# Splitting the heads while the recurrent stage still runs, the second norm made inside the output products, and first weights fetched ahead

## What is computed

```python
def _modulate(x, g, shift, scale):
    return _rmsnorm(x, g) * (1 + scale) + shift

def _hgrn_readout(o, gate, norm_g, w_out):
    o = _rmsnorm(o, norm_g)                       # per head
    o = o.reshape(o.shape[0], o.shape[1], E_WIDTH).astype(gate.dtype)
    return (o * jax.nn.silu(gate)) @ w_out        # 2048 -> 1024

def first_block(x, c, ...):
    ...
        x = x + gate[:, None] * y                 # y: the readout
    ...
        h = _modulate(x, norm_g[i], shift[:, None], scale[:, None])
    ...

def _conv_mixer(h, w_in, b_in, ...):
    p = h @ w_in + b_in                           # 1024 -> 3 * 2048
    a, gl, gate = jnp.split(p, 3, axis=-1)
    u = a * jax.nn.sigmoid(gl)
    ...
```

## Time and profile before

| | |
|---|---|
| median of 3 runs (lowest, highest) | 3842.87 us (3842.66, 3844.66) |
| the profiled execution | 3843.6 us |
| its span in the trace | 3841.7 us |
| PE busy in the span | 3545.6 us |
| mean granted clock of PE | 0.959 |

### The profile page before, as it was taken

The page is one execution under the profiler, slowest core; times in us unless marked ns, Lnnn a source line. Parts: engine busy times, 40 slices in busy tenths (PEclk is TensorE's granted clock), DMA queues, the critical chain, the costliest instruction groups (busy, mean ns, idle before and its releaser), DMA issues. The chain is left out here.

```text
span 3841.7 us, 57188 instructions
## 1 busy us (share of the span) xinstructions
PE 3545.6 (92%) x24387; PEld 2545.6 (66%) x24387; DVE 2026.4 (53%) x3153; ACT 1306.6 (34%) x2188; POOL 598.5 (16%) x316
## 2 busy tenths in 40 slices
PE   8999999997899989899999999999897978999998
PEld 5778778775444437554555547888575867878886
DVE  4157877773198885712133335333567575065422
ACT  4146665663211124521133223332343122333331
POOL 0000000002000000200000004444530001434442
PEclk9999999998999999999799999999898979999999
DMA  7622221222456560332021033332320002323332
GB/s 271 211 69 53 79 53 53 73 59 78 120 183 187 178 197 23 106 66 48 14 58 44 17 96 96 98 99 72 81 71 2 4 2 52 98 83 93 97 91 71
DMA packets 517587, 331.11 MB, mean 86 GB/s; under 512 B 31356, under 2 KB 493749, under 8 KB 517078
## 3 DMA queue, kind: packets, MB, share of 16 engines
q1 hardware_dynamic: 517334, 327.45, 29.5%
HBM read 316.93 MB, written 10.49 MB: 85 GB/s over the span
## 5 line engine op out<-in xcount | busy, mean ns | idle before, releaser
L1383 PE MATMUL cv_bank<-hT,cv_w 128*128 128x512 f32 x768 | 343.7, 601 | 13.7 <-DMA cv_w<-in_conv_w_in_dram 13.7
L3685 POOL TENSOR_TENSOR tl_wl<-tl_w,tl_wh 128x1024 fp32r<-128x1024 f32 (+1 forms) x104 | 246.2, 2368 | 679.0 <-ACT tl_wh L3798 678.8
L1534 DVE SCALAR_TENSOR_TENSOR conv_u<-cv_pad,vec,conv_u 128x512 f32<-128x512 f32 x480 | 319.2, 742 | 0.0
L1383 PEld LDWEIGHTS cv_bank<-hT,cv_w 128*128 128x128 f32 x768 | 143.3, 191 | 194.6 <-issue 180.2
L2498 POOL TENSOR_TENSOR mp_wl<-mp_w,mp_wh 128x1024 fp32r<-128x1024 f32 x72 | 173.1, 2407 | 592.9 <-ACT mp_wh L2572 592.9
L3798 ACT ACTIVATE tl_wh<-tl_w 128x1024 fp32r<-128x1024 f32 (+1 forms) x104 | 108.5, 1043 | 332.1 <-PE tl_bank L3722 329.9
L797 PE MATMUL hg_bank<-hg_hh,hg_wh 128*128 128x512 f32 x512 | 207.8, 406 | 4.6 <-PEq L194 4.6
L799 PE MATMUL hg_bank<-hg_hh,hg_wl 128*128 128x512 f32 x512 | 203.2, 397 | 0.0
L798 PE MATMUL hg_bank<-hg_hl,hg_wh 128*128 128x512 f32 x512 | 202.9, 396 | 0.0
L3720 PE MATMUL tl_bank<-tl_room,tl_wh 128*128 128x512 f32 x464 | 183.8, 396 | 11.7 <-POOL tl_wl L3685 10.9
L3722 PE MATMUL tl_bank<-tl_room,tl_wl 128*128 128x512 f32 x464 | 182.5, 393 | 0.0
(11 more groups left out here) (745 smaller groups left out, 8267.0 us busy)
## 6 DMA issues: line engine op xcount, KB each, us to landing
cv_ada<-in_w_ada_dram SPq DMA_DIRECT2D x48, 1024.0 KB, 7.7
hg_w<-in_hgrn_w_in_dram SPq DMA_DIRECT2D x64, 512.0 KB, 7.0
mp_w<-in_w_mlp_dram SPq DMA_DIRECT2D x64, 512.0 KB, 4.2
open_w<-in_ada_w_dram SPq DMA_DIRECT2D x12, 2048.0 KB, 9.8
cv_w<-in_conv_w_in_dram SPq DMA_DIRECT2D x48, 512.0 KB, 4.1
tl_w<-in_w_ffn_in_dram SPq DMA_DIRECT2D x44, 512.0 KB, 4.0
fr_w<-in_w_in_dram SPq DMA_DIRECT2D x26, 512.0 KB, 3.8
at_w<-in_w_in_dram SPq DMA_DIRECT2D x24, 512.0 KB, 4.0
```

Of the source, the lines that this page charges most:

```text
L1383: ins = pe.matmul(ps[n % RING][:, :], W[n % SLOTS][:, k * P:(k + 1) * P], K.hT[:, k, :], start=(k == 0), stop=(k == KD - 1))
L1534: ins = dve.scalar_tensor_tensor(o, x, by, o, ALU.mult, ALU.add)
L3685: pool.tensor_tensor(WL[u % SPLIT][:, 0:n, :], W[u % RAW][:, 0:n, :], WH[u % SPLIT][:, 0:n, :].bitcast(F32), ALU.subtract).then_inc(low, 1)
```

## The change

The splitting of heads 0 to 13 goes into hgrn_phase's last turn: ACT makes the high parts in three groups (`heads_high`) and POOL the low parts, into `ho_rh` and into the places of `hg_hl` and `ho_rl`. The weights of the first output tile are fetched in that stage too, ahead of SP's wait for the last projection. A new stage, heads_out_phase, takes the place of stream_phase("ho") and of norm_phase: it splits the first weights in four parts and the heads 14 and 15, makes the 8 output tiles as before, and beside them squares the new residual tiles (ACT) and adds the squares up (DVE), so that two matmuls with ones are left at its end, then the logarithm and the exponential. The scaling and the shift go to the start of conv_phase, one tile at a time, and the first product waits for each tile (`h_ok`). The convolution's first four weight tiles go to buffers of their own (`cv_first`), fetched in heads_out_phase behind the third output tile's weights.

```diff
@@ hgrn_phase, SP
+                sp.dma_start(K.hoW[:, :, :], inp["hgrn_w_out"][0].rearrange("(k p) n -> p k n", p=P)[:, :, 0:P]).then_inc(K.ho_in, 16)
                 sp.wait_ge(proj, NG * NH)
@@ hgrn_phase, POOL
+                for h in range(SPLIT_HEADS):
+                    pool.wait_ge(r_high, h + 1)
+                    o = K.hgL[:, h, :] if h < KD else K.hoL[:, h - KD, :]
+                    pool.tensor_tensor(o, hO[:, h, :], K.hoH[:, h, :].bitcast(F32), ALU.subtract).then_inc(r_low, 1)
@@ hgrn_phase, ACT
+                def heads_high(a, b):
+                    for h in range(a, b):
+                        act.wait_ge(fin_ok, h + 1)
+                        act.activation(K.hoH[:, h, :], hO[:, h, :], ACT.Copy).then_inc(r_high, 1)
...
                     log(1, h - 1)
+                    if h == NH:
+                        heads_high(0, 4)
...
                     turn(0, h - 1)
+                    if h == NH:
+                        heads_high(4, 9)
                     exps(1, h - 1)
+                    if h == NH:
+                        heads_high(9, SPLIT_HEADS)
...
-def stream_phase(K, tag, w, x, kt, iters, col, on_act, on_dve, freed_by, start=None):
...
+CONV_FIRST = [EW, 0, EW + P, P]
+def heads_out_phase(K):
+    SPLIT, BANKS, PARTS, ITERS = 2, 6, 4, KD
+    STEP = NH // PARTS
...
+                for u in range(1, ITERS):
+                    if u == 2:
+                        sp.wait_ge(part_low, PARTS)
+                    elif u > 2:
+                        sp.wait_ge(low, u - 2)
+                    sp.dma_start(W[u % 2][:, :, :], w[:, :, u * P:(u + 1) * P]).then_inc(w_in[u % 2], 16)
+                    if u == 2:
+                        sp.wait_ge(r_low, 2)
+                        for n, at in enumerate(CONV_FIRST):
+                            sp.dma_start(K.cvW[:, n, :].rearrange("q (k n) -> q k n", n=P), wc[:, :, at:at + P]).then_inc(K.cv_in, 16)
...
+                pe.wait_ge(added, KD - 1)
+                pe.matmul(SUM[:, :], K.ones[:, :], acc[:, :], start=True, stop=False)
+                pe.wait_ge(squared, KD)
+                pe.matmul(SUM[:, :], K.ones[:, :], sq[:, (KD - 1) % 2, :], start=False, stop=True).then_inc(sum_ok, 1)
...
+                act.wait_ge(K.ho_in, 16)
+                for c in range(PARTS):
+                    act.activation(WH[0][:, STEP * c:STEP * (c + 1), :], W[0][:, STEP * c:STEP * (c + 1), :], ACT.Copy).then_inc(part_high, 1)
+                for k in range(NH - 2, NH):
+                    act.activation(RH[:, k, :], K.hO[:, k, :], ACT.Copy).then_inc(r_high, 1)
+                weights_high(1)
+                act.preload_act_table_set(LOG_EXP_SET)
+                for u in range(ITERS):
+                    act.wait_ge(freed, u + 1)
+                    if u >= 2:
+                        act.wait_ge(added, u - 1)
+                    act.activation(sq[:, u % 2, :], K.xT[:, u, :], ACT.Square).then_inc(squared, 1)
                     weights_high(u + SPLIT)
...
@@ conv_phase, PE, ACT, DVE
                         for k in range(KD):
-                            ins = pe.matmul(ps[n % RING][:, :], W[n % SLOTS][:, k * P:(k + 1) * P], K.hT[:, k, :],
+                            if n == 0:
+                                pe.wait_ge(h_ok, k + 1)
+                            ins = pe.matmul(ps[n % RING][:, :], slot(n)[:, k * P:(k + 1) * P], K.hT[:, k, :],
...
+                for k in range(KD):
+                    act.wait_ge(h_mul, k + 1)
+                    act.activation(K.hT[:, k, :], K.hT[:, k, :], ACT.Identity, bias=K.mod[:, SHIFT + k, 0:1]).then_inc(h_ok, 1)
...
+                for k in range(KD):
+                    dve.scalar_tensor_tensor(K.hT[:, k, :], K.xT[:, k, :], gain[:, k:k + 1], K.hT[:, KD - 1, :],
+                                             ALU.mult, ALU.mult).then_inc(h_mul, 1)
...
-    norm_phase(K, [(K.xT, K.hT, T, K.at["norm_g"] + 8, 24, 32, 0)])
```

More of the change, by code:

```diff
@@ L130, in open_phase @@
         K.ctxL = K.sb(under, "ctx_hl", [P, KD, TC], F32R)
+    with ExitStack() as under:
+        K.hoL = K.sb(under, "ho_rl", [P, NH - KD, T], F32R)
     K.ctxT = K.sb(K.early, "ctxT", [P, KD, TC])
@@ L134, in open_phase @@
         slots = [K.sb(under, f"open_w{i}", [P, KD, GC]) for i in range(2)]
+    with ExitStack() as under:
+        K.cvW = K.sb(under, "cv_first", [P, len(CONV_FIRST), KD * P])
     K.hO = K.sb(K.early, "hgrn_out", [P, NH, T])
+    with ExitStack() as under:
+        K.hoH = K.sb(under, "ho_rh", [P, NH, T], F32R)
+    K.ho_in, K.cv_in = (K.ctx.enter_context(nc.semaphore(name)) for name in ("ho_first", "cv_first"))
     K.heads = ExitStack()
@@ L711, in hgrn_phase @@
          at_ok, kv_ok, s_ok, out_ok, sq_ok, ms_ok, ln_ok, rs_ok, o1_ok, fin_ok, back_ok) = sems[5:31]
-        high, low, x_back, half_ok = (K.ctx.enter_context(nc.semaphore(f"hg_sem{n}")) for n in range(4))
+        high, low, x_back, half_ok, r_high, r_low = (K.ctx.enter_context(nc.semaphore(f"hg_sem{n}")) for n in range(6))
+        SPLIT_HEADS = NH - 2
         GROUPS = [(ZF, 0), (ZF, 1), (ZB, 0), (ZB, 1), (Q, 0), (G, 0)]
@@ L1185, in weights_high @@
                 def weights_high(u):
-                    if u >= iters:
+                    if u >= ITERS:
                         return
-                    act.wait_ge(w_in[u % RAW], 16 * (u // RAW + 1))
+                    act.wait_ge(w_in[u % 2], arrived(u))
                     if u >= SPLIT:
                         act.wait_ge(summed, u - SPLIT + 1)
[L1191 to L1202, removed]
+                    act.activation(WH[u % SPLIT][:, :, :], W[u % 2][:, :, :], ACT.Copy).then_inc(high, 1)
+                act.wait_ge(K.ho_in, 16)
+                for c in range(PARTS):
+                    act.activation(WH[0][:, STEP * c:STEP * (c + 1), :], W[0][:, STEP * c:STEP * (c + 1), :], ACT.Copy).then_inc(part_high, 1)
@@ L1215, in _ @@
-                if start:
-                    start(dve, own)
-                for u in range(iters):
-                    if freed_by == "dve":
-                        dve.wait_ge(summed, u + 1)
-                    else:
-                        dve.wait_ge(freed, u + 1)
-                    on_dve(dve, u, ps[u % BANKS], freed, own)
+                for c in range(PARTS):
+                    dve.wait_ge(part_high, c + 1)
+                    part = slice(STEP * c, STEP * (c + 1))
+                    dve.tensor_tensor(WL[0][:, part, :], W[0][:, part, :], WH[0][:, part, :].bitcast(F32), ALU.subtract).then_inc(part_low, 1)
@@ new lines, in _ @@
+                for k in range(NH - 2, NH):
+                    dve.wait_ge(r_high, k - NH + 3)
+                    dve.tensor_tensor(RL(k), K.hO[:, k, :], RH[:, k, :].bitcast(F32), ALU.subtract).then_inc(r_low, 1)
+                for u in range(ITERS):
+                    dve.wait_ge(summed, u + 1)
+                    dve.scalar_tensor_tensor(K.xT[:, u, :], ps[u % BANKS][:, :], K.mod[:, 16 + u, 0:1], K.xT[:, u, :],
+                                             ALU.mult, ALU.add).then_inc(freed, 1)
+                    if u < KD - 1:
+                        dve.wait_ge(squared, u + 1)
+                        if u == 0:
+                            dve.tensor_copy(acc[:, :], sq[:, 0, :]).then_inc(added, 1)
+                        else:
+                            dve.wait_ge(added, u)
+                            dve.tensor_tensor(acc[:, :], acc[:, :], sq[:, u % 2, :], ALU.add).then_inc(added, 1)
@@ L1286, in conv_phase, with slot, landed @@
         ada_in = (ada_in0, ada_in1)
+        h_gain, h_mul, h_ok = (K.ctx.enter_context(nc.semaphore(f"conv_h_sem{n}")) for n in range(3))
+        def slot(n):
+            return K.cvW[:, n, :] if n < NF else W[(n - NF) % SLOTS][:, :]
+        def landed(n):
+            return (K.cv_in, 16 * NF) if n < NF else (w_in[(n - NF) % SLOTS], 16 * ((n - NF) // SLOTS + 1))
         grid = lambda t: t.rearrange("q (r t) -> q r t", t=GW)
@@ L1329, in _ @@
                         if n < 3 * NT_ + NT_:
[L1330 removed]
+                            if n >= SLOTS + NF:
+                                load(n)
                             n += 1
```

105 lines of the change are left out of this document (53 added, 52 removed).

## The result

The changed kernel takes 3823.84 us (median of 5 runs, 3822.29 to 3827.77) against 3842.66 (5 runs of the kernel before on the same chip, 3839.22 to 3844.66): a ratio of 0.9949, 95% interval 0.9938 to 0.9961. It is 0.5% faster. The profiled run took 3823.84, its span is 19.6 us shorter than before.

What follows compares the result with a forecast made beforehand. PE, busy 92% of the span, was taken as the bound, so only its waits could be won: 3843.6 - 10.6 - 19.7 + 9 = 3822.3 us, range 3814 to 3830.

Steps and rivals of the forecast that it cites:

- Norm and convolution's start: From last output product to first convolution product: 6.1 us instead of 25.75, as norm work is hidden; gain 19.7 us.
- Output projection's start: Heads already split and first weights fetched: PE starts about 1.3 us after the stage's start, not 11.89; gain 10.6 us.
- the two meet: Output projection: second tile's weights ready at 14.1 us, just as the first tile ends at 14.2, so no wait.
- The tail: Head 15 to the stage's end: POOL's low parts hold DVE, loss about 9 us, from 29.2 to 38 us.
- every second boundary: In head 15, POOL gets in at half of DVE's boundaries: 8 subtractions go ahead, at 1.1 us each.
- The upper bound of 13.7: Rival for head 15: POOL gets in at each DVE boundary, 13.7 us lost, 3827.0 us in all; chance 0.26.
- both slow starts: First output tile kept at 12.9 us and first convolution product 2.5 us slow, since PE's clock falls in waits.
- the main case: Whole kernel: loss of 6 to 12 us in head 15, time 3819 to 3826 us; chance 0.40.
- the wait of 4.5 us: Sign: PE's wait before the first output product should be some 4.5 us.
- three signs of being wrong: DVE's instructions as short as before, POOL running past DVE's last instruction, or the second output tile waiting for its weights.
- The rival without early start: Convolution's own weights come late, so only 10.6 us is won and 9 given back: 3842.0 us; chance 0.04.
- the slow one: Each POOL subtraction holds DVE far longer; at 2.85 us each, 39.9 us lost and 3853.2 us; chance 0.03.

Runs made afterwards that it cites:

- e5: The changed kernel with the convolution's first four weights loaded at the convolution's start again; 3833.85 us, ratio 0.9974.
- e6: The changed kernel's norm and convolution alone, with heads split and first weights loaded at the output projection's start as before the change; 3820.06 us, ratio 0.9942.
- e8: e1 plus the second output tile's weights fetched in head 15 and unread PE products filling PE's waits; 3809.95 us, ratio 0.9912.
- e1: The changed kernel with the heads' fourteen low parts made by DVE in its own waits of head 15 instead of by POOL; 3813.62 us, ratio 0.9924.
- e2: The changed kernel with POOL's fourteen subtractions released at three moments when DVE reads PSUM or waits; 3815.20 us, ratio 0.9930.
- e3: The changed kernel with each of POOL's fourteen subtractions made as two of 256 columns; 3822.59 us, ratio 0.9949.
- e4: The changed kernel with all sixteen heads split by ACT and DVE at the output projection's start, not in the tail; 3820.07 us, ratio 0.9945.
- e9: e8 with PE's unread products placed closer to the output projection's start, and one fewer at the convolution's start; 3811.35 us, ratio 0.9917.

## Why the prediction was right, step by step

The time came out 1.5 us above the forecast, inside the range, but that it came so close is luck: terms cancel. With the working's terms against the measured ones:

- **Norm and convolution's start**: 19.7 forecast, 19.6 measured; the 6.1 us were 6.15. Shown, by e5 and e6.
- **Output projection's start**: 10.6 forecast, 8.8 measured. PE did start 1.4 us after the stage's start. The first tile then took 13.5 us instead of 12.9 and ended at 14.92 instead of 14.2, and the step "the two meet" failed by a little: the second weights landed 8.6 us after the stage's start (916.93 - 908.32), not 7.6, since the DMA took 6.8 us from issue to landing and not 5.87 (why, no run shows); POOL ended at 923.51, PE waited 0.36 us for it, and tile 2 came 11.64 us after tile 1. e8, where it came after 10.93, shows that its weights were what was late. The other six tiles took 10.93 instead of 10.88.
- **The tail**: 9 forecast, 13.2 measured. This is the term that was mis-sized. The mechanism was right (e1, e2), and so was the price of 1.1 us for each subtraction that goes ahead. Wrong was "every second boundary": POOL got in at seven boundaries of seven from 868.87 on and at five from 885.55 on, 12 x 1.05 = 12.6 us; the last 0.6 is a wait of DVE for PE. The upper bound of 13.7, thirteen boundaries, to which I had given 0.26, was nearly the true case: twelve. The Trainium skill's page "SBUF — State Buffer", section "Who interferes with whom", with its exclusive lock for a whole instruction, was the better guide than my one row against it (910.57 in the earlier trace rows); the tail here agrees with it, 1.05 us of a 1.27 us instruction at each of twelve boundaries; only the first, at 867.74, POOL let pass.
- **The clock**: I kept both slow starts. The first product came down by 0.75, which is not shown to be the change's doing (with the same start it took 9.74 to 10.10 in e1, e3 and e4); e8 and e9 show that it is PE's waits ahead of a product that cost the rest.
- **The untouched stages**: I had nothing, 3.7 us came. That made up for most of the 5.3 us (21.3 forecast, 16.0 measured) that the touched stages fell short. Without it the time would have been 3827.6, in the range still, but at the rival's 3827.0 and not at the main case.

Of the signs I named, the wait of 4.5 us (4.61), the wait under 4 (3.56), DVE's instructions stretched by 1.1 us each (1.05) and the reads of PSUM that aren't held came; the tail was 42.4 instead of 38. For the second tile I had named some 13 us after the first: from end to end it was 11.64 (the working itself has 10.88 there), from start to start 13.84. And one of the three signs of being wrong came too, in small: the second output tile waited for its weights. The rival without early start and the slow one didn't come: the convolution's weights were there, and no 512-column subtraction held DVE for 2.85 us.

## What to carry to other kernels

An idle engine isn't free: here work put on POOL beside a chain of DVE instructions with two SBUF operands lengthened the chain by almost POOL's whole duration at each boundary. The same work beside reads of PSUM didn't hold DVE, as long as POOL's own queue was done in time (in e2 the tail was 3.2 us longer than before), and in DVE's own waits it cost the tail nothing. Before giving work to another engine, add up the waits of the one that is on the path: here DVE had 9 us of them in the very stretch. And split a large change: half of this one was worth the whole.

## What was not expected of the hardware

The stages behind the change run the same 16,538 matmuls in every kernel, and still took 2806.6 to 2811.3 us. Windows over them, changed kernel and e1, PE's busy time and the granted clock of one stretch within:

```profile
1015.47:3822.10 2806.63, 2617.09 (x16538) 1792.02 (x16536) 1419.32 (x2062) 795.68 (x1319) 561.53 (x290) 0.96 0.29 82
3045.00:3125.00 80.00, 50.20 (x688) 34.09 (x689) 59.58 (x98) 36.40 (x66) 0.00 (x0) 0.82 0.01 2
```
```profile
1001.87:3813.10 2811.23, 2621.90 (x16538) 1793.32 (x16536) 1419.30 (x2062) 795.92 (x1319) 562.17 (x290) 0.96 0.29 82
3031.50:3115.50 84.00, 56.45 (x688) 36.55 (x686) 58.66 (x96) 36.18 (x65) 0.00 (x0) 0.73 0.01 1
```

The difference is PE's: 4.8 us more busy time in e1. In one stretch of some 80 us where PE waits often it is 6.2 more, at a granted clock of 0.73 instead of 0.82; elsewhere it is a little less. What decides which it is in a run stays open. In the table the three kernels whose first product took 8.84 us (after, e2, e6) have the shortest rests, 2806.6 to 2807.0, and the five where it took 9.56 to 10.10 have 2810.3 and more; whether the two hang together wasn't tried. The difference is as large as several terms of the sum above, so a term of 4 us can be read from its stage and not from the whole.

Open too is why POOL's first instruction after some 650 us of idling let a boundary pass: it was recorded from 867.43, and DVE's scan at 867.74 still took its 1.22; the same is seen in e3 and, before, at 910.57. At 885.38, after 2.29 us of idling, it got in at the next boundary. The long idling alone doesn't do it: in e2 and e4 POOL came after 662 and 695 us, when DVE was reading PSUM or had nothing to do, and the next DVE instruction with two SBUF operands was held (874.19 and 906.39). The cause wasn't tried.
